# Four moves in one kernel: gate factors behind the third r tile, mixed tokens turned ahead of the S5 states, the last chunk's front half one half tile on, q tiles without the meta columns

## The chip, the cores and the metric

The kernel runs on one core of a Trainium2 chip. The metric is the device time of the whole program in microseconds (us), the median of several runs.

## What is computed

One layer of a hybrid decoder over 16 learned meta tokens, 256 prompt tokens and 8 sequences of 8 sample tokens (336 columns; 320 without the meta tokens, whose output is dropped), all in fp32:

```
xn   = rmsnorm(h) ; q, k, v, r, a, u = split(xn @ w_in)      # one input projection, width 2048 in
gk   = log_sigmoid(a @ w_gk2 + b_gk) / 16                    # GLA gates
o, S = gla_sequence(S0, q, k, v, gk)                         # chunked gated linear attention, 4 heads, dk 128, dv 256
o    = rmsnorm(o) * g_gla * silu(r)
y5   = s5_mix(u, ...)                                        # complex diagonal SSM, 64 groups
z    = gelu(y5) ; o5 = z * sigmoid(z @ w_glu + b_glu)
h    = h + concat(o, o5) @ w_out
h    = h + hier_moe(rmsnorm(h))                              # 32 experts 2048-512-2048, top 2 per token
y    = rmsnorm(h)
```

The outputs are y of prompt and sample tokens (the meta tokens' rows are dropped) and the new GLA and S5 states.

## The kernel before

Everything is laid out by hand in one SBUF array (`arena`) and one PSUM array (`ps`); each engine has its own instruction list, and semaphores order them.

**Input projection and mixers.** TensorE (PE) walks a list `TILES`: 8 u tiles, a, 4 q, 4 k, 8 v, 2 r (r0, r1), 4 gk, 6 r (r2 to r7), 8 glu. A tile is 128 output columns: `KT` = 16 weight blocks (8 for glu, 1 for gk) times all tokens, accumulated in PSUM bank p % 2. ScalarE (ACT) reads tile p out with `evacuate(p)`, and tile p + 2 waits for that. Tiles u, q, k, v have 336 columns, r and glu 320. The profile counts two PE instructions for one fp32 matmul. Weights arrive in two ring buffers of two tiles each (`load_chunk`, issued by SyncE, SP).

Between the halves of the tiles stand the steps of the S5 mixer and, from tile r5 on, those of the 11 GLA chunks (0 to 8 prompt, 9 and 10 sample; chunk 0 holds the meta tokens and gives no output). `GLA_FRONT[c]` and `GLA_BACK[c]` = front + 1 say at which half tile (2 x tile, or 2 x tile + 1) the chunk's two PE parts stand. `gla_front(c)` (L1940 to L1942) turns v and k and makes the scores; VectorE (DVE) then masks them and copies k in `front(c)` (L1452 to L1463). `gla_back(c)` (L1959, L1966, L1979) makes the output and the state updates, which DVE adds in `add_states(c)` (L1480). A sample chunk has four sequences: two updated in the back part, two in `sample_states(c, 2)` one half tile later. `gla_front(10)` waits until DVE has added all states of chunk 9. After a glu tile, DVE multiplies it into the mixed tokens with `gate_s5(i)` (L1486).

**Gates.** When gk tile 3 has been read, ACT runs `gates()`: Abs, Exp, Ln over 1408 columns; DVE takes the sums (L1411 to L1426); ACT makes `eb` and `en` (L1047, L1048); DVE takes differences (L1433 to L1437); ACT makes the last factor (L1050); DVE multiplies q and k (L1438 to L1442). All of it is one call in ACT's list, ahead of the evacuation of r2 and r3. Each change between Exp, Ln, Silu and Sigmoid costs ACT an ACT_TABLE_LOAD.

**End of the mixers.** ACT scales the ten output chunks (`scale_o`, L1066). PE turns the last S5 states `hl` (L2045, L2047), ACT copies them to `hlT` (L1107), and POOL stores them. Then PE turns the outputs chunk by chunk (L2058) and DVE multiplies them by `rT` (silu(r) times `ggla`, made at L1502) into `mixT` (L1511, 20 of them). Only then does the output projection start (L2096 and L2100, eight column blocks), with the residual rows `hrow` loaded by POOL's queue (L802 to L804) and added by DVE (L1520); PE turns h for the router between the blocks (`turn_h`, L2067, L2071).

**Experts.** The router follows. SP loads the 12 pieces of expert 0 during the output projection; each piece of a later expert is loaded when PE has used that piece of the expert before (`weights_used`, L547). All 32 experts (12 MB each) pass through the same 12 buffers (PE L2249 and L2290, DVE L1702).

Of the kernel before, what the change touches and what calls it, by code (L numbers as in the profile page):

```python
# [37 lines left out]
CL = 32  # L38
# [33 lines left out]
          + [("out", i) for i in range(8)])  # L72
CIDX = {c: i for i, c in enumerate(CHUNKS)}
COL0 = {"u": OFF_U, "q": OFF_Q, "k": OFF_K, "v": OFF_V, "r": OFF_R}
GLA_FRONT = [2 * TIDX[("r", 5)] + c for c in range(6)] + [2 * TIDX[("glu", c)] for c in range(5)]
GLA_BACK = [f + 1 for f in GLA_FRONT]


# [37 lines left out]
def bc(ap, axis, n):  # L116

    shape = list(ap.shape)
    assert shape[axis] == 1
    shape[axis] = n  # L120
    return ap.broadcast_to(shape)


def build(nc, A):
    ctx = ExitStack()
    with ctx:
# [458 lines left out]
        def _(pool):  # L585
# [90 lines left out]
            st(gp.tensor_tensor(par, p4[:, 0:2], p4[:, 2:4], ALU.add))  # L676

            for m in (qT, kT):
                st(gp.memset(m[:, 0, :, 0:PADT], 0.0))
            st(gp.memset(BP, 0.0))  # L680
            st(gp.memset(wgk, 0.0))
            st(gp.memset(wa[:, :, RANK:], 0.0))
# [204 lines left out]
        def _(act):  # L887
# [110 lines left out]
            def evacuate(p):  # L998
                kind, i = TILES[p]
                act.wait_ge(proj_done, p + 1)  # L1000
                src = ps[:, p % 2, 0:T]
                if kind == "u":
                    for q in range(4):
                        for t in range(LC):
                            u = sc.activation(U4[32 * t:32 * t + 32, i, q, :], ps[32 * q:32 * q + 32, p % 2, t:T:LC], ACT.Copy)  # L1005
                    u.then_inc(proj_read, 1)
                elif kind == "a":
                    act.wait_ge(xn_turned, 12)
                    sc.activation(aT, src, ACT.Copy).then_inc(proj_read, 1)
                elif kind in "qkv":  # L1010
                    if kind == "v" and i == 0:
                        act.wait_ge(xn_turned, 12)
                    if kind == "v":
                        h_, dst = i // 2, vT[:, i % 2].rearrange("p c (h i) -> p c h i", i=CL)
                    else:
                        h_, dst = i, qT if kind == "q" else kT
                    scale = DK ** -0.5 if kind == "q" else 1.0
                    st(sc.activation(dst[:, 0, h_, PADT:CL], src[:, 0:N_META], ACT.Copy, scale=scale))
                    sc.activation(dst[:, 1:, h_, :], src[:, N_META:].rearrange("p (c i) -> p c i", i=CL), ACT.Copy,
                                  scale=scale).then_inc(proj_read, 1)  # L1020
                elif kind == "gk":
                    act.wait_ge(scanned, 2 * NB)
                    act.wait_ge(hl_saved, 2 * NB)
                    act.wait_ge(vec_ready, 2)
                    st(sc.activation(bG[:, 0, i, PADT:CL], src[:, 0:N_META], ACT.Identity, bias=bgk[:, i:i + 1]))
                    sc.activation(bG[:, 1:, i, :], src[:, N_META:].rearrange("p (c i) -> p c i", i=CL), ACT.Identity,
                                  bias=bgk[:, i:i + 1]).then_inc(proj_read, 1)
                elif kind == "r":
                    sc.activation(rT[:, i, :], src[:, 0:TO], ACT.Silu).then_inc(proj_read, 1)  # L1029
                else:  # L1030
                    if i >= 2:
                        act.wait_ge(mix_s5, i - 1)
                    sc.activation(glu_t[i % 2], src[:, 0:TO], ACT.Sigmoid, bias=bglu[:, i:i + 1]).then_inc(proj_read, 1)

            def gates():
                act.wait_ge(rotated, 2 * NB)

                act.wait_ge(proj_read, TIDX[("gk", 3)] + 1)
                act.wait_ge(gate_b, 1)
                flat = [x.rearrange("p c h i -> p (c h i)") for x in (bG, eb, en)]  # L1040
                sc.activation(flat[2], flat[0], ACT.Abs).then_inc(gate_abs, 1)
                act.wait_ge(gate_abs, 1)
                sc.activation(flat[2], flat[2], ACT.Exp, scale=-1.0).then_inc(gate_abs, 1)
                act.wait_ge(gate_abs, 2)
                sc.activation(flat[2], flat[2], ACT.Ln, bias=1.0).then_inc(gate_abs, 1)
                act.wait_ge(gate_b, 3)
                sc.activation(flat[1], flat[0], ACT.Exp, scale=1.0 / 16).then_inc(gate_exp, 1)  # L1047
                sc.activation(flat[2], flat[2], ACT.Exp, scale=-1.0 / 16).then_inc(gate_exp, 1)  # L1048
                act.wait_ge(gate_b, 5)
                sc.activation(flat[0], flat[0], ACT.Exp, scale=1.0 / 16).then_inc(gate_exp, 1)  # L1050
# [17 lines left out]
            for p in range(len(TILES)):  # L1068
# [25 lines left out]
                    act.wait_ge(o_sqrt, 1)  # L1094
                    sc.activation(gss[:, 0:NCH - 1], gss[:, 0:NCH - 1], ACT.Sqrt).then_inc(o_sqrt, 1)
                evacuate(p)
                if TILES[p] == ("glu", 6):
                    act.wait_ge(o_rstd, 1)
                    scale_o(range(5))
                if TILES[p] == ("glu", 7):  # L1100
                    scale_o(range(5, NCH - 1))
                if TILES[p] == ("gk", 3):
                    gates()
            for i in range(2):

                act.wait_ge(hl_turned, i + 1)
                sc.activation(hlT[:, 3 * i:3 * i + 3, :], ps[:, 2 + i, 0:384].rearrange("p (a b) -> p a b", b=128),  # L1107
                              ACT.Copy).then_inc(hl_copied, 1)
# [92 lines left out]
        def _(dve):  # L1201
# [260 lines left out]
                else:  # L1462
                    ve.tensor_copy(Kexp[:, 0], ps[:, f, 256:384]).then_inc(front_ready, 1)  # L1463

            def add_states(c):
                sample = c >= NCP
                for s_ in range(SPC if sample else 1):
                    dve.wait_ge(st_done, st_count(c) + (4 * (s_ // 2) + 3 + s_ % 2 if sample else 2))
                    for h_ in range(H):
                        b_, at = state_bank(c, s_, h_)  # L1470
                        if sample:
                            dst = sstate[c - NCP][:, s_, h_]
                            dcol = eb[:, c, h_, DSEQ * s_ + DSEQ - 1:DSEQ * s_ + DSEQ]
                        else:
                            dst, dcol = S[:, h_], eb[:, c, h_, CL - 1:CL]
                        if c == 0 and h_ == 0:
                            dve.wait_ge(masks_made, 3)
                        if h_ == 0 and c >= 1:
                            dve.wait_ge(st_added, 2 * st_count(c))
                        ve.scalar_tensor_tensor(out=dst, in0=dst, scalar=dcol, in1=ps[:, b_, at:at + DV], op0=ALU.mult,  # L1480
                                                op1=ALU.add).then_inc(st_added, 1)
# [3 lines left out]
                dve.wait_ge(z_ready, 1)  # L1485
                ve.tensor_tensor(mixT[:, 8 + c, :], glu_t[c % 2], zT[:, c, :], ALU.mult).then_inc(mix_s5, 1)  # L1486

            for c in range(NCH):
                front(c)
                add_states(c)  # L1490
                kind, i = TILES[GLA_FRONT[c] // 2]
                if kind == "glu":
                    gate_s5(i)
            dve.wait_ge(o_read, NCH - 1)
            g10 = gss[:, 0:NCH - 1]
            ve.tensor_scalar(g10, g10, 1.0 / DV, EPS, ALU.mult, ALU.add).then_inc(o_sqrt, 1)
            gate_s5(5)
            dve.wait_ge(o_sqrt, 2)
            ve.reciprocal(gss[:, 16:16 + NCH - 1], g10).then_inc(o_rstd, 1)

            dve.wait_ge(proj_read, TIDX[("r", 7)] + 1)
            st(ve.tensor_tensor(rT, rT, bc(ggla.unsqueeze(2), 2, TO), ALU.mult))  # L1502
            gate_s5(6)
            gate_s5(7)
            st.sync()
            for c in range(NCH - 1):
                for hf in range(2):
# [332 lines left out]
        def _(pe):  # L1840
# [163 lines left out]
            for p, (kind, i) in enumerate(TILES):  # L2004
# [17 lines left out]
                for k in range(kt):  # L2022
# [11 lines left out]
                        mm = te.matmul(out, wgk[:, DK * i:DK * i + DK], aT, start=True, stop=True)  # L2034
                    else:
                        w = ring[n % 2][:, 0:256 * kt].rearrange("p (k n) -> p k n", n=256)[:, k, 128 * (i % 2):128 * (i % 2) + 128]
                        x = zT[:, k, :] if kind == "glu" else xnT[:, k, N_META:T] if kind == "r" else xnT[:, k, :]
                        o = out if kind not in ("r", "glu") else out[:, 0:TO]
                        mm = te.matmul(o, w, x, start=(k == 0), stop=(k == kt - 1))  # L2039
                mm.then_inc(proj_done, 1)  # L2040

            pe.wait_ge(hl_saved, 2 * NB)
            pe.wait_ge(st_added, 2 * st_count(NCH))
            for r_ in range(2):
# [3 lines left out]
                                      hl[:, r_, 1 + 4 * m:5 + 4 * m, :].rearrange("p s j -> p (s j)"), ident)  # L2048
                mm.then_inc(hl_turned, 1)

            pe.wait_ge(hl_copied, 2)
            for c in range(NCH - 1):
                pe.wait_ge(o_scaled, c + 1)
                for hf in range(2):
                    n = 2 * c + hf
                    if n >= 4:
                        pe.wait_ge(mix_gla, n - 3)
                    te.transpose(ps[:, XB[n % 4], 0:128], o_all[:, c, 128 * hf:128 * hf + 128], ident).then_inc(o_turned, 1)  # L2058

            def turn_h(i):  # L2060

                if i:
                    pe.wait_ge(hnT_ready, 2 * i)
                pe.wait_ge(h_added, 3 * i + 2)
                for k in range(2):
                    for t in range(2):
# [279 lines left out]
```

## Time and profile before

| | |
|---|---|
| median of 3 runs | 1602.82 us (1602.67 to 1604.31) |
| profiled execution | 1603.32 us, its span 1600.1 us |
| granted TensorE clock, mean | 0.882 of full speed |
| PE busy | 1263.1 us (79%) |
| DVE, ACT, POOL busy | 455.8, 255.1, 93.6 us |
| DMA | 486.60 MB, mean 304 GB/s |
| chain that ended last | PE 51%, DMA 40%, DVE 3%, issue 2%, ACT 2% |

The span runs from the first to the last instruction of the profiled execution, and its time is that of the whole program. Shares are averages over stages with different limits. The chain that ended last is followed back from the last instruction, at each step to what released it. A value in brackets behind an instruction in order of time is the idle time of its engine ahead of it and what ended that. PEld is TensorE's weight load, which overlaps its matmuls. The granted clock is a share of 2.4 GHz; its two levels are 1.2 and 2.4 GHz.

### The profile page before, as it was taken

The numbers are of one execution on the slowest core, as the hardware profiler recorded it, in microseconds if no ns is written. First come the engines' busy times: TensorE is split into PE (matmuls) and PEld (weight loads), VectorE is DVE, ScalarE is ACT, GpSimd is POOL, SyncE is SP. The second block draws the span as 40 slices with busy tenths as digits, with TensorE's granted clock in tenths as the row PEclk, the third lists the DMA queues.
The fourth block names the chain that finished last, engine by engine and source line by source line (L and its number), as shares of the span: only waits on it lengthen the run. The fifth ranks groups of instructions, "written<-read, shape, count | busy, mean of one in ns | idle before, by whom it ended". The sixth has DMA issues, their size and how long they took to land.

```text
span 1600.1 us, 17678 instructions
## 1 busy us (share of the span) xinstructions
PE 1263.1 (79%) x7026; PEld 681.2 (43%) x7026; DVE 455.8 (28%) x993; ACT 255.1 (16%) x692; POOL 93.6 (6%) x259
## 2 busy tenths in 40 slices
PE   5999999999989995866766766767766766665857
PEld 4667777765568884322222222222222222222222
DVE  4167667232430004302201201201211211201314
ACT  5452232443121112000000000000000000000012
POOL 6700000100010002000000000000000000000000
PEclk9999999999999997778878977877887887878988
DMA  9331333251379533799999999999999999999996
GB/s 214 107 106 59 100 106 102 66 156 53 106 238 368 217 106 107 315 426 429 427 428 428 428 428 428 425 428 430 418 429 428 424 430 427 422 423 426 394 426 286
DMA packets 110790, 486.60 MB, mean 304 GB/s; under 512 B 17940, under 2 KB 83288, under 8 KB 83656
## 3 DMA queue, kind: packets, MB, share of 16 engines
q1 hardware_dynamic: 107592, 473.09, 74.1%
q0 software_dynamic: 2848, 12.61, 2.4%
q8 instruction: 43, 0.70, 0.2%
q14 instruction: 19, 0.16, 0.0%
q10 hardware_dynamic: 288, 0.04, 0.0%
HBM read 478.42 MB, written 10.78 MB: 306 GB/s over the span
## 4 chain that ended last, share of the span: by engine, by line
PE 51%; DMA 40%; DVE 3%; issue 2%; ACT 2%; SPq 1%; POOL 0%; POOLq 0%; DVEq 0%; ACTq 0%
DMA arena<-in_w_up 39%; PE ps L2039 19%; PE ps L2249 11%; PE ps L2096 7%; PE ps L2195 4%; PE ps L2100 2%; PE ps L2290 1%; PE ps L1979 1%; DVE arena L1685 1%; PE ps L1914 1%; PE ps L1902 1%; SPq L547 1%; PE ps L2273 1%; DMA arena<-in_x_sample 1%; DMA hn_rows<-arena 1%
## 5 line engine op out<-in xcount | busy, mean ns | idle before, releaser
L2249 PE MATMUL ps<-arena 128*32 128x512 f32 x2048 | 321.1, 774 | 215.8 <-DMA arena<-in_w_up 214.4
L2039 PE MATMUL ps<-arena 128*128 128x336 f32 (+1 forms) x1152 | 331.1, 445 | 4.9 <-ACT arena L1029 3.6
L2249 PEld LDWEIGHTS ps<-arena 128*32 128x32 f32 x2048 | 81.2, 136 | 446.0 <-issue 445.3
L2039 PEld LDWEIGHTS ps<-arena 128*128 128x128 f32 x1152 | 216.1, 191 | 103.5 <-issue 5.8
L2290 PE MATMUL ps<-arena 128*32 128x512 f32 x1024 | 148.9, 733 | 22.7 <-DVE arena L1709 19.1
L1702 DVE COPY arena<-ps 128x512 f32<-128x512 f32 x31 | 21.3, 688 | 397.4 <-PE ps L2249 397.4
L1145 ACT ACTIVATE arena<-ps 128x128 f32<-128x128 f32 x32 | 8.9, 278 | 705.8 <-PE ps L2273 705.8
L2096 PE MATMUL ps<-arena 128*128 128x256 f32 x512 | 114.5, 382 | 0.6 <-issue 0.6
L2195 PE MATMUL ps<-arena 128*128 128x512 f32 (+3 forms) x192 | 103.0, 666 | 7.0 <-DVE arena L1685 5.1
L2096 PEld LDWEIGHTS ps<-arena 128*128 128x128 f32 x512 | 96.0, 190 | 14.9 <-issue 2.0
L1685 DVE TENSOR_TENSOR arena<-arena,ps 128x1024 f32<-128x1024 f32 (+1 forms) x48 | 58.4, 1218 | 137.1 <-PE ps L2195 137.1
L2290 PEld LDWEIGHTS ps<-arena 128*32 128x32 f32 x1024 | 39.4, 131 | 115.5 <-issue 107.7
L2273 PE MATMUL ps<-arena 128*128 128x64 f32 x256 | 66.3, 405 | 22.8 <-DVE arena L1702 22.0
L2273 PEld LDWEIGHTS ps<-arena 128*128 128x128 f32 x256 | 62.1, 327 | 41.6 <-DVE arena L1702 39.9
L1723 DVE COPY arena<-ps 32x512 f32<-32x512 f32 x62 | 42.8, 691 | 117.8 <-PE ps L2290 116.8
L1152 ACT ACTIVATE arena<-ps 32x512 f32<-32x512 f32 x62 | 36.4, 587 | 180.8 <-PE ps L2290 180.0
L2195 PEld LDWEIGHTS ps<-arena 128*128 128x128 f32 (+3 forms) x192 | 30.9, 180 | 71.7 <-issue 40.9
L872 POOL DMA_INDIRECT arena<-hn_rows,arena x7 | 7.0, 994 | 728.8 <-DVE arena L1705 728.8
L995 ACT ACTIVATE arena<-ps 32x80 f32<-32x80 f32 x128 | 39.2, 306 | 30.6 <-PE ps L1914 29.2
L1480 DVE SCALAR_TENSOR_TENSOR arena<-arena,ps 128x256 f32<-128x256 f32 x68 | 27.8, 475 | 55.4 <-PE ps L1979 55.4
L1520 DVE TENSOR_TENSOR arena<-arena,ps 128x256 f32<-128x256 f32 x16 | 6.6, 421 | 114.3 <-PE ps L2096 94.9
L1005 ACT ACTIVATE arena<-ps 32x84 f32<-32x84 f32 x128 | 29.7, 232 | 46.4 <-PE ps L2039 45.0
(387 smaller groups left out, 942.9 us busy)
## 6 DMA issues: line engine op xcount, KB each, us to landing
arena<-in_w_gate SPq DMA_DIRECT2D x62, 2048.0 KB, 18.4
arena<-in_w_up SPq DMA_DIRECT2D x62, 2048.0 KB, 22.8
arena<-in_w_down SPq DMA_DIRECT2D x62, 2048.0 KB, 22.0
arena<-in_w_in SPq DMA_DIRECT2D x16, 2048.0 KB, 9.0
arena<-in_w_out SPq DMA_DIRECT2D x8, 2048.0 KB, 8.5
arena<-in_state_gla SPq DMA_DIRECT2D x8, 512.0 KB, 9.0
arena<-in_w_glu SPq DMA_DIRECT2D x4, 1024.0 KB, 5.1
out_new_gla_sample<-arena SPq DMA_DIRECT2D x2, 2048.0 KB, 21.6
```

Of the source, the lines that this page charges most:

```text
L995: y = sc.activation(at, ps[32 * i:32 * i + 32, YB[c % 2], NCO * q:NCO * q + NCO], ACT.Copy)
L1005: u = sc.activation(U4[32 * t:32 * t + 32, i, q, :], ps[32 * q:32 * q + 32, p % 2, t:T:LC], ACT.Copy)
L1152: sc.activation(Os[CAP * i:CAP * i + CAP, 512 * x:512 * x + 512], ps[CAP * x:CAP * x + CAP, 6 + i % 2, :], ACT.Copy).then_inc(out_a, 1)
L1685: ve.tensor_tensor(d_, d_, ps[0:TR[t], b_:b_ + 2, :].rearrange("p b c -> p (b c)"), ALU.add)\
L1723: ve.tensor_copy(Os[CAP * i:CAP * i + CAP, 512 * x:512 * x + 512], ps[CAP * x:CAP * x + CAP, 6 + i % 2, :]).then_inc(out_b, 1)
L2039: mm = te.matmul(o, w, x, start=(k == 0), stop=(k == kt - 1))
L2096: mm = te.matmul(ps[:, OB[i % 2][t], 0:256], mixT[:, m, 128 * t:128 * t + 128], w[:, m, :], start=(m == 0), stop=(m == 15))
L2100: mm = te.matmul(ps[NS * x:NS * x + NS, OB[i % 2][t], 0:128], mixT[:, m, SEQ:TO], w[:, m, 128 * x:128 * x + 128], start=(m == 0), stop=(m ...
L2195: mm = te.matmul(ps[0:TR[t], b_ + x, :], Wsel[rows, 128 * t:128 * t + TR[t]], Os[rows, 1024 * j + 512 * x:1024 * j + 512 * x + 512], start ...
L2249: mm = te.matmul(ps[CAP * x:CAP * x + CAP, 0, :], xT[:, 4 * q + at, CAP * i:CAP * i + CAP], wpiece[4 * (q // 2) + 2 * up + q % 2][:, HID * ...
L2273: mm = te.matmul(ps[:, 1, at:at + 2 * CAP], GUs[:, k:HID:4], fold2.rearrange("p x t -> p (x t)"), start=True, stop=True)
L2290: mm = te.matmul(ps[CAP * x:CAP * x + CAP, 6 + i % 2, :], HT[:, k, :], wpiece[8 + k][:, 512 * x:512 * x + 512], start=(k == 0), stop=(k == 3))
```

## The change

Five edits. The gate factors (from the wait for `gate_b` on) become `gate_factors()`, called behind the evacuation of r2. Chunk 10's front part moves from the start of tile glu4 to its middle, its back part to the start of glu5, and its last states to the middle of glu5; DVE's list follows: only two sequences' states of chunk 10 ahead of the norm of the outputs, the rest behind it, and `scale_o` one tile earlier. The product of `rT` with `ggla` moves from behind the norm to behind `gate_s5(0)`. The turning of the outputs moves ahead of the turning of the S5 states, which now stands ahead of its last pair. The q tiles are computed and read for 320 columns; q of chunk 0 is set to zero.

```diff
-GLA_FRONT = [2 * TIDX[("r", 5)] + c for c in range(6)] + [2 * TIDX[("glu", c)] for c in range(5)]
+GLA_FRONT = [2 * TIDX[("r", 5)] + c for c in range(6)] + [2 * TIDX[("glu", c)] for c in range(4)] + [2 * TIDX[("glu", 4)] + 1]
...
-                st(gp.memset(m[:, 0, :, 0:PADT], 0.0))
+                st(gp.memset(m[:, 0, :, 0:CL if m is qT else PADT], 0.0))
...
+                    if kind == "q":
+                        sc.activation(qT[:, 1:, i, :], src[:, 0:TO].rearrange("p (c i) -> p c i", i=CL), ACT.Copy,
+                                      scale=DK ** -0.5).then_inc(proj_read, 1)
+                        return
...
+            def gate_factors():
+                flat = [x.rearrange("p c h i -> p (c h i)") for x in (bG, eb, en)]
                 act.wait_ge(gate_b, 3)
...
-                if TILES[p] == ("glu", 6):
+                if TILES[p] == ("glu", 5):
                     act.wait_ge(o_rstd, 1)
                     scale_o(range(5))
-                if TILES[p] == ("glu", 7):
+                if TILES[p] == ("glu", 6):
                     scale_o(range(5, NCH - 1))
                 if TILES[p] == ("gk", 3):
                     gates()
+                if TILES[p] == ("r", 2):
+                    gate_factors()
...
-            for c in range(NCH):
+            for c in range(NCH - 1):
                 front(c)
                 add_states(c)
                 kind, i = TILES[GLA_FRONT[c] // 2]
                 if kind == "glu":
                     gate_s5(i)
+                    if i == 0:
+                        st(ve.tensor_tensor(rT, rT, bc(ggla.unsqueeze(2), 2, TO), ALU.mult))
+            front(NCH - 1)
+            add_states(NCH - 1, range(2))
             dve.wait_ge(o_read, NCH - 1)
...
-            gate_s5(5)
+            gate_s5(4)
             dve.wait_ge(o_sqrt, 2)
             ve.reciprocal(gss[:, 16:16 + NCH - 1], g10).then_inc(o_rstd, 1)
-
-            dve.wait_ge(proj_read, TIDX[("r", 7)] + 1)
-            st(ve.tensor_tensor(rT, rT, bc(ggla.unsqueeze(2), 2, TO), ALU.mult))
-            gate_s5(6)
-            gate_s5(7)
+            add_states(NCH - 1, range(2, SPC))
+            for i in range(5, 8):
+                gate_s5(i)
...
-                        x = zT[:, k, :] if kind == "glu" else xnT[:, k, N_META:T] if kind == "r" else xnT[:, k, :]
+                        x = zT[:, k, :] if kind == "glu" else xnT[:, k, N_META:T] if kind in "qr" else xnT[:, k, :]
...
+            pe.wait_ge(st_added, 2 * st_count(NCH))
+            for c in range(NCH - 1):
+                pe.wait_ge(o_scaled, c + 1)
+                for hf in range(2):
+                    n = 2 * c + hf
+                    if n >= 4:
+                        pe.wait_ge(mix_gla, n - 3)
+                    te.transpose(ps[:, XB[n % 4], 0:128], o_all[:, c, 128 * hf:128 * hf + 128], ident).then_inc(o_turned, 1)
+
+            pe.wait_ge(mix_gla, 2 * (NCH - 1) - 2)
             pe.wait_ge(hl_saved, 2 * NB)
             pe.wait_ge(st_added, 2 * st_count(NCH))
...
-            pe.wait_ge(hl_copied, 2)
-            for c in range(NCH - 1):
...
                 if i:
                     pe.wait_ge(hnT_ready, 2 * i)
+                else:
+                    pe.wait_ge(hl_copied, 2)
```

## Rows read from the trace of the kernel before

**Rows 1.** Busy time per engine in three stretches; last columns clock, DMA share, GB/s.

```profile
200.00:300.00 100.00, 100.00 (x496) 72.64 (x495) 65.02 (x153) 32.12 (x111) 0.00 (x0) 1.00 0.29 89
...
500.00:550.00 50.00, 50.00 (x381) 43.35 (x378) 3.81 (x11) 5.78 (x22) 0.00 (x0) 1.00 0.87 324
...
656.00:1590.00 934.00, 655.94 (x3662) 236.52 (x3662) 185.01 (x305) 56.95 (x110) 6.96 (x7) 0.82 1.00 424
```

**Rows 2.** Chain that ended last, expert 0 and the weight stream.

```profile
650.53 3.61 PE ps L2249 x32
...
654.72 21.21 DMA arena<-in_w_up
```

**Rows 3.** Who TensorE waited for, 310 to 470 us: total, times, longest.

```profile
PE ps L2039 <- ACT arena L1029: 3.6, 1, 3.6
PE ps L1940 <- DVE arena L1480: 3.0, 1, 3.0
PE ps L2058 <- ACT arena L1107: 2.7, 1, 2.7
```

**Rows 4.** Chain that ended last, three halves of tiles of 336 columns.

```profile
119.36 13.60 PE ps L2039 x48
```

**Rows 5.** Instructions in order of time around the gates.

```profile
320.31 17.41 PE L2039 MATMUL ps<-arena 128*128 128x320 f32 x64
...
328.28 1.28 ACT L1047 ACT_TABLE_LOAD   x1
...
334.67 1.38 ACT L1047 ACTIVATE arena<-arena 128x1408 f32<-128x1408 f32 x1 [5.10 <-DVEq L1426]
...
341.20 1.62 DVE L1442 TENSOR_TENSOR arena<-arena 128x1408 f32<-128x1408 f32 x1
...
341.31 4.04 PE L2039 MATMUL ps<-arena 128*128 128x320 f32 x14 [3.60 <-ACT arena L1029]
```

**Rows 6.** Instructions in order of time, second glu tile (GLA chunk 7).

```profile
402.07 0.49 DVE L1486 TENSOR_TENSOR arena<-arena 128x320 f32<-128x320 f32 x1 [1.24 <-ACT arena L1033]
...
402.68 0.28 DVE L1463 COPY arena<-ps 128x128 f32<-128x128 f32 x1
...
404.11 0.70 PE L1979 MATMUL ps<-arena 32*128 32x256 f32 x4
```

**Rows 7.** Instructions in order of time, chunk 10 and the last glu tiles.

```profile
431.57 0.66 PE L1940 MATMUL ps<-arena 128*128 128x128 f32 x2 [2.98 <-DVE arena L1480]
...
432.66 3.47 PE L2039 MATMUL ps<-arena 128*128 128x320 f32 x8
...
443.15 1.90 PE L1979 MATMUL ps<-arena 32*128 32x256 f32 x16 [0.54 <-DVE arena L1480]
...
444.99 13.19 PE L2039 MATMUL ps<-arena 128*128 128x320 f32 x48
```

**Rows 8.** Instructions in order of time, last glu tiles to output projection.

```profile
451.03 2.76 DVE L1502 TENSOR_TENSOR arena<-arena 128x2560 f32<-128x2560 f32 x1
...
458.21 0.53 ACT L1033 ACTIVATE arena<-ps,arena 128x320 f32<-128x320 f32 x1 [1.79 <-PE ps L2039]
...
458.77 0.49 DVE L1486 TENSOR_TENSOR arena<-arena 128x320 f32<-128x320 f32 x1 [3.81 <-ACT arena L1033]
...
461.96 4.59 DVE L1511 TENSOR_TENSOR arena<-ps,arena 128x128 f32<-128x128 f32 x20 [2.70 <-PE ps L2058]
...
466.66 8.65 PE L2096 MATMUL ps<-arena 128*128 128x256 f32 x39 [0.60 <-issue]
```

**Rows 9.** Busy time per engine and granted clock in two stretches.

```profile
432.00:436.00 4.00, 4.00 (x14) 2.90 (x13) 1.79 (x6) 0.39 (x1) 0.00 (x0) 0.63 0.00 0
...
461.00:466.00 5.00, 4.25 (x20) 3.01 (x20) 4.00 (x18) 1.96 (x4) 3.28 (x6) 0.66 1.05 349
```

**Rows 10.** Instructions in order of time, first residual add and first turn of h.

```profile
485.95 0.75 DVE L1520 TENSOR_TENSOR arena<-arena,ps 128x256 f32<-128x256 f32 x2 [19.40 <-DMA arena<-in_x_sample]
...
491.29 0.60 PE L2067 MATMUL ps<-arena 128*128 128x128 f32 x4
```

More of the change, by code:

```diff
@@ L1015, in evacuate @@
                     else:
[L1016 to L1020, printed above, removed]
+                        h_, dst = i, kT
+                    st(sc.activation(dst[:, 0, h_, PADT:CL], src[:, 0:N_META], ACT.Copy))
+                    sc.activation(dst[:, 1:, h_, :], src[:, N_META:].rearrange("p (c i) -> p c i", i=CL), ACT.Copy)\
+                      .then_inc(proj_read, 1)
                 elif kind == "gk":
@@ L1463, in front, with add_states @@
                     ve.tensor_copy(Kexp[:, 0], ps[:, f, 256:384]).then_inc(front_ready, 1)
-            def add_states(c):
+            def add_states(c, which=None):
                 sample = c >= NCP
-                for s_ in range(SPC if sample else 1):
+                for s_ in which or range(SPC if sample else 1):
                     dve.wait_ge(st_done, st_count(c) + (4 * (s_ // 2) + 3 + s_ % 2 if sample else 2))
@@ L2036, in _ @@
                         w = ring[n % 2][:, 0:256 * kt].rearrange("p (k n) -> p k n", n=256)[:, k, 128 * (i % 2):128 * (i % 2) + 128]
-                        x = zT[:, k, :] if kind == "glu" else xnT[:, k, N_META:T] if kind == "r" else xnT[:, k, :]
-                        o = out if kind not in ("r", "glu") else out[:, 0:TO]
+                        x = zT[:, k, :] if kind == "glu" else xnT[:, k, N_META:T] if kind in "qr" else xnT[:, k, :]
+                        o = out if kind not in ("q", "r", "glu") else out[:, 0:TO]
                         mm = te.matmul(o, w, x, start=(k == 0), stop=(k == kt - 1))
                 mm.then_inc(proj_done, 1)
+            pe.wait_ge(st_added, 2 * st_count(NCH))
[7 more added lines that the diff above has]
+            pe.wait_ge(mix_gla, 2 * (NCH - 1) - 2)
             pe.wait_ge(hl_saved, 2 * NB)
@@ L2049, in _ @@
                 mm.then_inc(hl_turned, 1)
-            pe.wait_ge(hl_copied, 2)
-            for c in range(NCH - 1):
[L2053 to L2058, printed above, removed]
             def turn_h(i):
```

## The prediction

> **What bounds the kernel.** I began with the busy times by stretch. From 656 to 1590 us the DMA engines are full at 424 GB/s while PE is idle a third of the time; in the projections, 200 to 300 us, PE is busy throughout and the DMA engines are not, and so it is in the output projection [rows 1]. Two stages with two limits, so the next question is what ties them. The chain that ended last shows it: 32 passes of expert 0 end at 654.14, and 0.58 us later a transfer of expert 1 starts, which is on the chain for 21 us [rows 2]. The weight stream can't start before expert 0 frees its pieces, and expert 0 stands at the end of PE's list: projections, GLA, output projection, router. So a microsecond that PE gains ahead of the output projection moves the whole stream, and the end, by a microsecond; nothing gained on DVE or ACT counts unless PE waited for it. The waits of PE between 310 and 470 us are therefore the list to look at: 3.6 us for ACT's read of an r tile, 3.0 for DVE's states, 2.7 for ACT's copy of the S5 states [rows 3]. The sum below is the shift of the start of L2096, 466.66 us before [rows 8].
>
> **q tiles.** Four tiles of 16 matmuls, two passes each, go from 336 to 320 columns: 128 passes. A pass of 336 columns takes 13.60 / 48 = 0.283 us [rows 4], one of 320 columns 17.41 / 64 = 0.272 us [rows 5]; 128 x 0.0113 = 1.4 us. By columns alone it would be 0.283 x 16 / 336 x 128 = 1.7. PE is never idle in 200 to 300 us [rows 1], and the q tiles stand in the same S5 pattern, so I count it in full: 1.4, ends 0 (DVE's S5 chain sets the pace after all) and 1.7. The memset that is wider by 16 columns a head runs on POOL while PE turns x and is counted at nothing: without that cover it is a fraction of a microsecond.
>
> **Gate factors.** PE ends r3 at 320.31 + 17.41 = 337.72 and starts r4 at 341.31: 3.6 us [rows 5], the longest wait [rows 3]. r4 needs r2 read; r2 was done at 320.31 + 8.7 = 329.0, but ACT was inside the gates until the last factor at 338.1 and a table load behind it. With the new list ACT, free at 328.3, loads Silu's table (1.28, as the row at 328.28 [rows 5]), reads r2 (0.45) at 329.6 to 330.0, loads Exp's table again until 331.3, and only then waits for DVE's sums, which come at 334.67 as before. The added table load lies in that wait with 3.3 us over; without the wait it would cost 1.3. Behind it everything runs as before: last factor 338.1, r3 read at 341.3. r4 starts at 337.7, ends at 346.4; r5 needs r3 read (341.3) and the first GLA front part needs DVE's last product (341.20 + 1.6 = 342.8 [rows 5]): both are there 3.6 us or more before. Queued behind ACT's new wait is only the read of r3, which stood behind the same wait before. Gain 3.6; ends 0 and 3.6.
>
> **Product of rT.** It takes 2.76 us [rows 8]. Before, it ran from 451.03 while ACT had not yet read glu6, so taking it from there gains nothing. Behind `gate_s5(0)` it stands ahead of DVE's front part of chunk 7: gate_s5 is at 402.07, so the product runs from about 402.5 to 405.2 and the copy of k, at 402.68 before, comes 2.7 us later, ending at 405.7. PE's back part of chunk 7 started at 404.11 [rows 6] and now waits until about 405.7: a new stall of 1.6 us inside glu1, with the rest of PE's list behind it. -1.6; ends -2.8 (nothing covers it) and 0.
>
> **Chunk 10.** DVE ends chunk 9's states at about 431.4, and `gla_front(10)` starts at 431.57 [rows 7] after 3.0 us of waiting [rows 3]. Now half of glu4 (8 passes, 8 x 0.272 = 2.2 us) is put ahead of it; 0.8 us of the wait is left. So 2.2 us of work goes into the wait. The granted clock then: the front part took 432.66 - 431.57 = 1.09, and the next eight passes 3.3 us against 2.2 (0.63 granted in 432 to 436) [rows 7, 9]; in both PE came out of the 3.0 us wait at the lower level, 1.2 GHz for about 3 us. With the wait cut to 0.8 us I expect the upper level: 0.5 + 1.1 = 1.6 us back. The rest of the pattern (back part, half a tile, 0.5 us wait for DVE, four states, 443.15 to 444.99 for the last [rows 7]) keeps its length and is followed by two and a half tiles where three stood. Gain 2.2 + 1.6 = 3.8; ends 2.2 (clock still low) and 4.0. On DVE the norm's two small steps and a later `add_states` fit in front of glu5's end. ACT reads glu5 after the root and a table load, some 2 us ahead of the end of glu5, and glu7 needs it a tile later.
>
> **Turning.** glu7 ended at 444.99 + 13.19 = 458.18; L2096 started at 466.66, 8.5 us later. In between: S5 states turned (to 458.8), 2.7 us wait for ACT, which was at `scale_o` and then the copies, then 20 products on DVE in 4.6 us [rows 3, 8]. Now the outputs are scaled before glu7 ends, and the first product waits only for ACT's read of glu7 (0.56) and `gate_s5(7)` (to 459.26, 1.1 us after PE's end [rows 8]). 1.1 + 4.6 = 5.7 to the last product. The S5 states' turning (0.65 us) waits for the 18th, 0.46 us before that, so L2096 starts about 6.1 us after glu7. Gain 8.5 - 6.1 = 2.4; ends 1.0 (see the clock below) and 2.8. Its queues: SP's list here (weights of block 1, then the stores of the GLA states) hangs on glu7's end as before and passes no moved step. ACT's copy of the S5 states and POOL's six stores come 3 us later, and ahead of the residual rows in POOL's list; POOL was waiting there for the store of S anyway, and is about even with it. The first residual add was at 485.95, PE's first turn of h, which needs it, at 491.29 [rows 10]. PE comes 2.4 us earlier relative to that load: 2.9 us are left, about 2.1 after the two adds. The wait for ACT's copy of the S5 states, which stood ahead of the turning, now stands ahead of that first turn of h, some 25 us after the copy. Expert 0's pieces have the whole output projection and router to arrive.
>
> **Sum.** 1.4 + 3.6 - 1.6 + 3.8 + 2.4 = 9.6 us. The profiled execution took 1603.3 us, so one like it takes 1593.7; it lay 0.5 above the median of 1602.8, and I predict 1593.2 us for the median, 0.6% less.
>
> **The clock, row and rule.** Between 461 and 466 us the granted clock was 0.66 after PE had waited 2.7 us, and the output projection began at the upper level: 39 passes in 8.65 us, 0.22 each [rows 9, 8]. The sum takes that for after too. The Trainium skill, "TensorE: Matmul & The Clock Gate", Part 1, says that the clock is throttled by default and activity releases it; the rows at 431 and 461 us agree. By that rule the change has a weak place: ahead of L2096 PE now does nothing but turnings at DVE's pace for 6 us. By the row, 2.4 us is gained there; by the rule it may be some 1.5 less, if the low level lasts into L2096 as it lasted 3 us in [rows 7]. That is a rival.
>
> **Rivals.** *Low clock into the output projection*, or after chunk 9's states: costs 1 to 3 us, time 1594.2 to 1596.2. For it: the two low stretches [rows 9]. Against: after such a stretch L2096 started at full level. Chance 0.17. *Residual rows late*: column block 2's weights are now asked for 2.4 us earlier and share the DMA engines with the rows' last microseconds; 2 us of margin could become a stall of up to 2 us: 1593.2 to 1595.2, chance 0.06. *The r4 wait stays* (ACT enters the Exp load late or r3's read slips): 1596.8, chance 0.04. *The rT product is hidden*, because DVE reaches it earlier or PE has other work: 1591.6, chance 0.08; against it, PE's own list has nothing else at that place. *The stream gives it back*: it starts earlier but takes longer. 9.6 of 934 us is 1%, while the DMA share is already 1.00 [rows 1]; within 0.2% it would have to give back 6.4 us: 1600 to 1605, chance 0.04. *Slower*: the output projection stays at 1.2 GHz after the turnings. Each pass then costs 0.22 us more [rows 8]; 44 passes eat the 9.6 us, 58 or more give over 1606, and the projection has 512 of them and as many narrower ones. Against: the lower level lasted 3 us in both places. Chance 0.01. My forecast, all five terms within their neighbourhood (1591.7 to 1594.7), holds the remaining 0.60.
>
> The range takes in all but the last two rivals: 1590.5 to 1597. A measurement of this kernel can tell about 0.2% (3.2 us) from no change. Faster 0.94, within 0.2% 0.04, slower 0.02 (0.01 added for what I haven't seen).
>
> **What would show it.** Right: q passes of 0.272 us; r4 behind r3 without a gap, and a Silu and an Exp load between Ln and L1047; a wait of PE for DVE of about 1.6 us in glu1 and the rT product ahead of it; under 1 us ahead of `gla_front(10)`, clock 1.0 behind it; about 6 us from glu7's end to L2096; L2096 at about 457 us and expert 1's first transfers 9.6 us earlier. Wrong: a longer first wait for the residual rows, slow passes at the start of L2096, or a stream longer than 945 us from the first transfer to the end.

## The result and the profile after

The changed kernel took 1592.97 us (median of 6 runs, 1591.46 to 1595.3), the kernel before 1603.57 us in the same comparison (6 runs): ratio 0.9928, 95% interval 0.9914 to 0.9941. The profiled execution took 1591.46 us; its span is 1589.7 us, 10.4 shorter than before. Runs more than 1.5% above the fastest of their kernel count in no ratio of this document; there were two, both of rt_twice below (1688.77 and 4929.36 us, of ten).

The waits of TensorE (PE) from 305 to 465 us: total, times, longest. L2044, L2049, L2059 and L2109 are the old L2034, L2039, L2058 and L2096.

```profile
PE ps L1989 <- issue: 1.6, 1, 1.6
PE ps L1989 <- DVE arena L1488: 1.1, 2, 0.5
PE ps L2059 <- DVE arena L1521: 1.0, 1, 1.0
PE ps L2044 <- ACT arena L1032: 0.7, 1, 0.7
PE ps L1950 <- DVE arena L1488: 0.6, 1, 0.6
```

Of the three waits of [rows 3] the one of 3.6 us is gone and the one of 3.0 is 0.6. The 2.7 us for ACT's copy are gone too; in the turnings PE now waits 1.0 us for DVE's first product. The wait of 1.6 us "for issue" is new. The 0.7 us and the two of 0.5 were there before.

The q tiles, in the chain that ended last, and instructions in order of time around the gates:

```profile
119.63 12.96 PE ps L2049 x48
```

```profile
319.09 26.02 PE L2049 MATMUL ps<-arena 128*128 128x320 f32 x96
...
327.06 1.28 ACT L1032 ACT_TABLE_LOAD   x1
...
328.35 0.44 ACT L1032 ACTIVATE arena<-ps 128x320 f32<-128x320 f32 x1
328.81 1.28 ACT L1053 ACT_TABLE_LOAD   x1
...
333.41 1.38 ACT L1053 ACTIVATE arena<-arena 128x1408 f32<-128x1408 f32 x1 [3.32 <-DVEq L1434]
...
339.95 1.62 DVE L1450 TENSOR_TENSOR arena<-arena 128x1408 f32<-128x1408 f32 x1
...
344.95 0.27 PE L1950 MATMUL ps<-arena 128*128 128x128 f32 x1
```

48 passes of the q tiles take 12.96 us for 13.60 [rows 4]. From the first pass of the q tiles to the second half of the first k tile it is 48.68 us (113.26 to 161.94) where 50.38 stood (112.78 to 163.16). r2, r3 and r4 are one row of 96 passes. ACT loads Silu's table, reads r2, loads Exp's table and stands ready 3.3 us before DVE's sums let it go on, at 333.41. DVE's last product ends at 341.6, 3.4 us before the first GLA front part (344.95).

Second glu tile:

```profile
396.99 0.49 DVE L1494 TENSOR_TENSOR arena<-arena 128x320 f32<-128x320 f32 x1 [1.25 <-ACT arena L1036]
397.40 2.82 DVE L1503 TENSOR_TENSOR arena<-arena 128x2560 f32<-128x2560 f32 x1
...
400.33 0.28 DVE L1471 COPY arena<-ps 128x128 f32<-128x128 f32 x1
...
400.72 0.70 PE L1989 MATMUL ps<-arena 32*128 32x256 f32 x4 [1.62 <-issue]
```

The rT product stands between `gate_s5(0)` and chunk 7's front part, whose last copy ends at 400.6; PE had been free for 1.6 us.

Chunk 10 and the end of the glu tiles; then the way to the output projection:

```profile
425.13 2.42 PE L2049 MATMUL ps<-arena 128*128 128x320 f32 x8
...
428.18 0.41 PE L1950 MATMUL ps<-arena 128*128 128x128 f32 x2 [0.63 <-DVE arena L1488]
...
428.76 2.32 PE L2049 MATMUL ps<-arena 128*128 128x320 f32 x8
...
438.14 1.90 PE L1989 MATMUL ps<-arena 32*128 32x256 f32 x16 [0.54 <-DVE arena L1488]
...
439.97 11.03 PE L2049 MATMUL ps<-arena 128*128 128x320 f32 x40
```

```profile
451.04 0.53 ACT L1036 ACTIVATE arena<-ps,arena 128x320 f32<-128x320 f32 x1 [1.79 <-PE ps L2049]
...
451.60 0.49 DVE L1494 TENSOR_TENSOR arena<-arena 128x320 f32<-128x320 f32 x1 [3.81 <-ACT arena L1036]
452.01 4.04 DVE L1521 TENSOR_TENSOR arena<-ps,arena 128x128 f32<-128x128 f32 x20
...
452.44 3.20 PE L2059 MATMUL ps<-arena 128*128 128x128 f32 x16 [1.00 <-DVE arena L1521]
...
455.71 0.28 PE L2065 MATMUL ps<-arena 128*32 128x128 f32 x1
...
456.38 13.98 PE L2109 MATMUL ps<-arena 128*128 128x256 f32 x64
```

Eight passes of glu4 now stand ahead of chunk 10's front part, eight behind it at 0.27 us each. glu7 ends at 439.97 + 11.03 = 451.00. The first product of DVE starts 1.0 us later, 20 take 4.04 us, and the S5 states turn from 455.71 on, under the last of them.

The clock in three of these stretches (the number before the DMA share), 0.63 and 0.66 in the stretches of [rows 9]:

```profile
428.00:432.00 4.00, 3.82 (x27) 2.59 (x31) 2.22 (x8) 0.91 (x2) 0.00 (x0) 1.00 0.00 0
...
451.00:454.00 3.00, 2.00 (x13) 1.31 (x11) 2.40 (x12) 0.53 (x1) 0.00 (x0) 1.00 0.58 173
454.00:456.30 2.30, 2.23 (x15) 1.66 (x15) 2.05 (x11) 0.05 (x1) 0.00 (x0) 1.00 1.06 367
```

The first residual add and PE's first turn of h; then the weight stream:

```profile
479.37 0.75 DVE L1530 TENSOR_TENSOR arena<-arena,ps 128x256 f32<-128x256 f32 x2 [23.31 <-DMA arena<-in_x_sample]
...
480.94 0.60 PE L2080 MATMUL ps<-arena 128*128 128x128 f32 x4
```

```profile
644.19 0.39 SPq L547 DMA_DIRECT2D arena<-in_w_up  x1
...
646.00:1580.00 934.00, 649.31 (x3660) 234.10 (x3659) 185.27 (x306) 56.96 (x110) 6.96 (x7) 0.82 1.00 423
```

5.3 us stood between the two before [rows 10], 1.6 us now, 0.8 after the second add: nothing waited. The second pair of expert 1's transfers is issued at 644.19 us, before at 654.72 [rows 2]: 10.5 us earlier. The stream is as full as before [rows 1].

To compare traces I cut each profiled execution at five places that the timeline shows: the first pass of r2, PE's front part of chunk 0, the end of glu7, the start of the output projection, and expert 0's first pass. In us:

| | start to r2 | r2 to front 0 | to end of glu7 | to projection | to expert 0 | to end | span |
|---|---|---|---|---|---|---|---|
| before | 320.3 | 29.7 | 108.2 | 8.5 | 177.7 | 955.7 | 1600.1 |
| after | 319.1 | 25.9 | 106.1 | 5.4 | 177.6 | 955.8 | 1589.7 |
| gates_only | 323.2 | 25.9 | 107.9 | 8.4 | 177.6 | 955.7 | 1598.7 |
| gates_only_2 | 321.0 | 25.9 | 108.2 | 8.5 | 177.8 | 955.9 | 1597.3 |
| q_only | 318.4 | 29.8 | 108.2 | 8.5 | 177.6 | 955.9 | 1598.3 |
| chunk10_only | 321.1 | 31.4 | 104.4 | 8.0 | 177.7 | 955.2 | 1597.7 |
| turn_only | 324.2 | 32.5 | 108.8 | 5.4 | 177.6 | 956.4 | 1604.8 |
| chunk10_back | 317.8 | 25.9 | 111.5 | 5.4 | 177.6 | 956.1 | 1594.2 |
| rt_twice | 321.6 | 25.9 | 112.9 | 5.4 | 177.6 | 956.8 | 1600.1 |
| rt_hidden | 319.0 | 25.9 | 104.4 | 5.4 | 177.6 | 957.2 | 1589.4 |
| rt_hidden_hl_early | 318.9 | 25.9 | 104.4 | 5.2 | 177.7 | 960.9 | 1592.9 |
| r4_filled | 321.2 | 29.6 | 108.1 | 8.5 | 177.5 | 955.9 | 1600.8 |
| after_2 | 319.4 | 25.9 | 106.1 | 5.4 | 177.5 | 956.0 | 1590.2 |
| rt_hidden_2 | 319.9 | 25.9 | 104.4 | 5.4 | 177.6 | 956.6 | 1589.7 |

Each row is one execution, so a stage that agrees over many rows can be read to 0.1 us, and a span only to a few us. The stage from the projection to expert 0 is the same to 0.3 us in all fourteen.

### The profile page after: what moved, and what is told of

It is laid out like the page before. It is cut to its first block, busy times and chain, and to the rows that moved or that the text cites. A ratio compares the mean times of both kernels' runs of the same rounds, so it can differ in the third digit from the quotient of the medians.

```text
span 1589.7 us, 17676 instructions
## 1 busy us (share of the span) xinstructions
PE 1252.5 (79%) x7026; PEld 677.4 (43%) x7026; DVE 455.4 (29%) x993; ACT 256.4 (16%) x689; POOL 93.5 (6%) x259
## 4 chain that ended last, share of the span: by engine, by line
PE 55%; DMA 37%; DVE 3%; issue 2%; SPq 1%; ACT 1%; POOL 0%; POOLq 0%; DVEq 0%; ACTq 0%
DMA arena<-in_w_up 35%; PE ps L2049 20%; PE ps L2262 11%; PE ps L2109 7%; PE ps L2208 5%; PE ps L2303 2%; PE ps L2113 2%; DVE arena L1695 1%; PE ps L1989 1%; PE ps L2286 1%; PE ps L1924 1%; PE ps L1912 1%; DMA arena<-in_x_sample 1%; SPq L547 1%; DMA hn_rows<-arena 1%
## 5 line engine op out<-in xcount | busy, mean ns | idle before, releaser
L2049 PE MATMUL ps<-arena 128*128 128x336 f32 (+1 forms) x1152 | 328.2, 442 | 1.3 <-issue 1.3
L2049 PEld LDWEIGHTS ps<-arena 128*128 128x128 f32 x1152 | 215.3, 190 | 97.5 <-issue 3.7
L2109 PE MATMUL ps<-arena 128*128 128x256 f32 x512 | 114.4, 382 | 0.0
L2109 PEld LDWEIGHTS ps<-arena 128*128 128x128 f32 x512 | 96.0, 190 | 14.1 <-issue 1.2
L1005 ACT ACTIVATE arena<-ps 32x84 f32<-32x84 f32 x128 | 29.7, 232 | 46.4 <-PE ps L2049 45.0
```

The costliest lines, as they stand in the source:

```text
L2109: mm = te.matmul(ps[:, OB[i % 2][t], 0:256], mixT[:, m, 128 * t:128 * t + 128], w[:, m, :], start=(m == 0), stop=(m == 15))
```

## The experiments

Theory: every microsecond that PE waits or works less ahead of expert 0 comes off the end, and each part of the change is worth its own PE time. Rivals: the stream gives it back; the waits hide each other; the clock, not the wait, is what changed. The ratio behind a label is that to the kernel before on the same chip, with its 95% interval.

**Gates alone** (gates_only, gates_only_2): the kernel before with

```diff
+            def gate_factors():
+                flat = [x.rearrange("p c h i -> p (c h i)") for x in (bG, eb, en)]
                 act.wait_ge(gate_b, 3)
...
+                if TILES[p] == ("r", 2):
+                    gate_factors()
```

> The kernel before with the gate factors behind the read of r2, and nothing else of the change. My theory: r4 starts behind r3 without a gap (3.6 us before), and since nothing later in the list takes it up, the output projection, expert 1's first transfer and the end all come 3.6 to 3.9 us earlier: about 0.23% faster. Rival, the weight stream has its own start or gives the time back: the output projection starts earlier but the span stays within 1 us.

> Gate factors alone once more, beside r4_filled on one chip. My theory: the wait's 3.6 us and the clock of r4_filled together, so 4 to 6 us (0.25 to 0.37%) shorter than before, and 3.6 us shorter than r4_filled. Rival, exactly the wait: 3.6 us, and r4_filled as long as before.

0.995 (0.9933 to 0.9967), then 0.9974 (0.9961 to 0.9987). Front part 0 comes 25.9 us behind r2 in both, 3.9 us less than before, and nothing later in the table grows. The second interval, 2.1 to 6.3 us, holds the 3.9; the first (four runs), 5.3 to 10.8, lies above it, and nothing in its trace explains the excess. The second holds my 4 to 6 us and the rival's 3.6 alike, so it does not part them.

**q tiles alone** (q_only): the memset, the evacuation and the matmul lines of the change.

> The kernel before with only the q tiles cut to 320 columns. My theory: passes of 0.270 us for 0.283, 128 of them, so the gk tiles and everything behind start 1.7 us earlier and the span is 1.7 us shorter. Rival, DVE's S5 chain sets the pace between the q tiles: PE shows waits for DVE or ACT ahead of the S5 parts and the span is shorter by less than 0.5 us.

0.9992 (0.9968 to 1.0016): within noise, as 1.7 us are 0.1%. Its start to r2 is 1.9 us shorter than before's, but this stage differs by up to 3.9 us between executions with equal q tiles (table). So the size rests on the pass, (13.60 - 12.96) / 48 x 128 = 1.7 us, and on the stretch of the q tiles: 48.68 us here too (112.57 to 161.25), 1.7 less than before. The mean start to r2 is 321.8 us over the six traces with the old q tiles and 319.3 over the eight with the new: the right way, and 1.7 within that spread. The profile shows no new wait of PE between the q tiles.

**Chunk 10 alone** (chunk10_only): `GLA_FRONT`, DVE's list with `gate_s5(4)`, then the last states, then the rT product as before, then `gate_s5` 5 to 7.

> The kernel before with only chunk 10's parts half a tile on (PE's places and DVE's list; the rT product stays behind the norm, scale_o and the turnings stay). My theory: wait ahead of the front part 0.6 to 0.8 us for 3.0, granted clock 1.0 behind it, the end of glu7 3.8 us earlier. From there as before unless the rT product, now behind chunk 10's last states, delays gate_s5: span 3.5 to 3.8 us shorter. Rival, the clock does not come back: only 2.2 us, with passes of 0.53 us after the front part.

0.9977 (0.9965 to 0.9989). The interval, 1.8 to 5.6 us, holds the forecast; the rival's 2.2 is ruled out by the trace: the stage to the end of glu7 is 104.4 us, 3.8 shorter, as in the sum, with 2.2 us for the eight passes behind the front part. A by-product is in the next stage, 0.5 us shorter with the turnings unchanged: the 20 products of DVE took 4.05 us there, not 4.59 [rows 8], with PE at the upper level (granted clock 1.00, in [rows 9] 0.66).

```profile
460.71 4.05 DVE L1514 TENSOR_TENSOR arena<-ps,arena 128x128 f32<-128x128 f32 x20 [2.71 <-PE ps L2061]
...
459.70:464.70 5.00, 3.87 (x20) 2.62 (x20) 3.99 (x20) 2.01 (x4) 3.28 (x6) 1.00 1.08 352
```

**Turnings alone** (turn_only): the outputs turned ahead of the S5 states, `scale_o` a tile earlier.

> The kernel before with only the turnings exchanged and scale_o one tile earlier. My theory from the trace of after: PE stays at the upper level of the clock, the 20 products take 4.0 us for 4.6, the S5 states turn under the last of them, and the output projection starts 5.4 us after the end of glu7 for 8.5: 3.1 us shorter. Rival, the faster products in the trace of after came from something else of the change: products at 0.23 us each here too, 2.4 us shorter.

0.9972 (0.9955 to 0.9989), that is 1.8 to 7.2 us. 5.4 us from glu7 to the projection, 3.1 shorter, and 4.04 us for the 20 products: the rival with 0.23 us each falls. Together with chunk10_only this splits the term: 0.5 us from the products at the upper level, 2.6 from the order. The profiled execution was nevertheless 4.7 us longer than before's. The table says where: start to r2 (3.9) and r2 to front 0 (2.8), neither touched by this edit. Its r tiles, in order of time, and the clock behind the wait:

```profile
324.17 17.41 PE L2039 MATMUL ps<-arena 128*128 128x320 f32 x64
...
345.32 11.56 PE L2039 MATMUL ps<-arena 128*128 128x320 f32 x32 [3.74 <-ACT arena L1029]
...
345.30:350.30 5.00, 4.98 (x10) 3.18 (x11) 1.53 (x1) 0.29 (x1) 0.00 (x0) 0.50 1.09 356
```

The 32 passes of r4 behind the 3.7 us wait take 11.39 us to the front part (345.32 to 356.71), at a granted clock of 0.50 in the first 5 us, against 8.72 in [rows 5] (341.31 to 350.03), which had nearly the same wait (3.60) and a clock of 1.00. And its first u tile took 12.3 us where before's took 9.3. The same wait is followed by slow passes in one execution and not in another.

**Chunk 10 put back** (chunk10_back): the changed kernel with `GLA_FRONT` and the order of DVE's `front`, `add_states` and `gate_s5` for chunk 10 of before.

> The changed kernel with chunk 10's parts back at their places of before, all else kept. My theory: the wait of 3.0 us ahead of the front part returns, the clock falls to the lower level for about 3 us, and the span is 3.8 us longer than the changed kernel's (1593.5). Rival, clock unharmed: 2.2 us longer.

0.9937 (0.9917 to 0.9956). The stage to the end of glu7 is 111.5 us, 5.5 longer than after, more than the 3.8 I expected and far more than the rival's 2.2. The run times can't settle that size: the ratio is 0.0009 above the changed kernel's 0.9928, 1.4 us, and the two intervals together leave 3.8 us either way.

```profile
399.38 0.70 PE L1985 MATMUL ps<-arena 32*128 32x256 f32 x4 [1.62 <-issue]
...
401.90 4.01 PE L2045 MATMUL ps<-arena 128*128 128x320 f32 x8
...
428.49 0.41 PE L1946 MATMUL ps<-arena 128*128 128x128 f32 x2 [2.98 <-DVE arena L1488]
...
429.09 3.99 PE L2045 MATMUL ps<-arena 128*128 128x320 f32 x8
```

Behind the 3.0 us wait eight passes take 3.8 us where 2.2 would do (429.09 to 432.91, granted clock 0.57 from 429 to 433), so the clock falls. But eight passes behind the product's 1.6 us wait take 3.9 us as well, 1.6 more than in the changed kernel's trace. Chunk 10's own part is as expected: from the second state updates of chunk 9 to the end of glu7 it is 31.5 us, 27.7 in the changed kernel. 3.8 + 1.6 = 5.4.

**The rT product** (rt_twice, rt_hidden, rt_hidden_2): doubled in place by a product without use (first cut), and moved into a gap of DVE (second):

```diff
                     if i == 0:
                         st(ve.tensor_tensor(rT, rT, bc(ggla.unsqueeze(2), 2, TO), ALU.mult))
+                        st(ve.tensor_tensor(mixT[:, 0:8], zT, bc(ggla.unsqueeze(2), 2, TO), ALU.mult))
```

```diff
                 front(c)
+                if c == 6:
+                    dve.wait_ge(proj_read, TIDX[("r", 7)] + 1)
+                    st(ve.tensor_tensor(rT, rT, bc(ggla.unsqueeze(2), 2, TO), ALU.mult))
                 add_states(c)
...
-                    if i == 0:
-                        st(ve.tensor_tensor(rT, rT, bc(ggla.unsqueeze(2), 2, TO), ALU.mult))
```

> The changed kernel with a second product of the same size (zT by ggla, into a part of the mixed tokens that is overwritten later) right behind the rT product. The output is the reference's; the second product is work without use. My theory: PE's wait in glu1 grows by the whole 2.7 us to 4.3 and so does the span (1592.4), since PE's list ahead of expert 0 is the limit; perhaps 1 us more if the clock falls to the lower level in that wait. Rival, something behind takes it up: span within 1 us of the changed kernel.

> The changed kernel with the rT product between front(6) and add_states(6), where DVE waited 3.3 us for PE. My theory: the 1.6 us wait of PE in glu1 was all due to the product's place; it goes, and the span is 1.6 to 1.7 us shorter than that of the changed kernel (about 1588.0). Rival, the product's cost is only moved: DVE's states of chunk 6 come late and PE waits as long in the next part.

Doubled: 0.9962 (0.9948 to 0.9976). Against the changed kernel's ratio that is 5.5 us longer, 2.3 to 8.6 with both intervals: nothing behind takes it up. The stage grew by 6.9 us: the wait by 2.7, as expected, and the rest is clock. The clock behind the wait, then instructions in order of time:

```profile
405.98:414.80 8.82, 8.82 (x26) 4.47 (x27) 1.66 (x4) 0.75 (x3) 0.00 (x0) 0.50 0.01 2
```

```profile
405.98 1.22 PE L1990 MATMUL ps<-arena 32*128 32x256 f32 x4 [4.36 <-issue]
...
410.46 4.54 PE L2050 MATMUL ps<-arena 128*128 128x320 f32 x8
...
415.38 2.32 PE L2050 MATMUL ps<-arena 128*128 128x320 f32 x8
```

From 405.98 to 414.8 PE works at half speed (granted clock 0.50); the 8 passes of 2.2 us take 4.4. I had expected "perhaps 1 us" of that, and it was 4.1.

Hidden: 0.9903 (0.9882 to 0.9924).

```profile
390.48 0.28 DVE L1471 COPY arena<-ps 128x128 f32<-128x128 f32 x1
390.68 2.81 DVE L1500 TENSOR_TENSOR arena<-arena 128x2560 f32<-128x2560 f32 x1
...
394.02 1.66 DVE L1488 SCALAR_TENSOR_TENSOR arena<-arena,ps 128x256 f32<-128x256 f32 x4 [0.53 <-PE ps L1990]
```

The product fits into DVE's wait for PE's state updates, 3.3 us before; 0.5 us of it is left, the states start as before, and PE's wait in glu1 is gone: 104.4 us for 106.1 in the table, in both runs. On one chip with the changed kernel:

> The changed kernel once more, on the chip of the next. Expected: 0.6 to 0.75% shorter than before; u0, r4 and glu passes at the upper level in this profile or some 3 us more where one of them is not.

> rt_hidden once more, on the chip of the changed kernel. My theory: 1.7 us shorter than the changed kernel, and up to 1 us more in the mean, since the wait of 1.6 us in glu1 was followed by slow passes in one trace (chunk10_back). Rival: no difference that shows beyond 0.5 us.

after_2 0.9934 (0.9912 to 0.9955), median 1592.05 us; rt_hidden_2 0.9916 (0.9899 to 0.9933), median 1590.09. Both expectations of size hold in the medians: 0.66% for the changed kernel, and 2.0 us between the two, which agree with the stage's 1.7. But the intervals overlap, and the profiled spans differ by only 0.3 us (rt_hidden, after) and 0.5 us (the second pair): in both traces of rt_hidden the stretch behind expert 0's first pass is longer, 957.2 and 956.6 us for 955.8 and 956.0. It is 955.2 to 956.8 in the traces of slower kernels as well, so whether the stream gives part of these 1.7 us back, or differs by itself, is not shown.

**S5 states turned in DVE's last wait** (rt_hidden_hl_early): rt_hidden with

```diff
+                    if n == 4:
+                        pe.wait_ge(hl_saved, 2 * NB)
+                        for r_ in range(2):
+                            te.transpose(ps[0:NJ, 4 + 3 * r_, 0:128], hl[:, r_, 0, :], ident)
...
```

> The kernel rt_hidden with the S5 states turned in the 1.0 us in which PE waits for DVE's first product, into banks 4 and 7. My theory: their 0.65 us fit into that wait, the output projection starts 0.2 to 0.3 us earlier relative to glu7's end, POOL's stores and the residual rows are issued earlier; about 1.9 us shorter than the changed kernel (1587.8). Rival, the states' turning pushes the later turnings and the projection starts as late or later.

0.9903 (0.9882 to 0.9924), the same as rt_hidden beside it; a gain of 0.2 us can't be seen in a ratio. The stage is 0.2 us shorter, as expected. But the residual rows did not come earlier for PE. Instructions in order of time:

```profile
449.40 0.27 PE L2061 MATMUL ps<-arena 128*32 128x128 f32 x1
...
450.47 3.29 PE L2068 MATMUL ps<-arena 128*128 128x128 f32 x16 [0.25 <-DVE arena L1522]
...
454.27 14.05 PE L2109 MATMUL ps<-arena 128*128 128x256 f32 x64 [0.51 <-issue]
...
477.62 0.75 DVE L1531 TENSOR_TENSOR arena<-arena,ps 128x256 f32<-128x256 f32 x2 [23.45 <-DMA arena<-in_x_sample]
...
478.91 0.60 PE L2078 MATMUL ps<-arena 128*128 128x128 f32 x4
```

PE's turn of h starts 0.5 us behind the end of the first two adds, 0.8 in the changed kernel. POOL had issued its six stores by 454.4 us and then waited 5.8 us for the store of S: the rows hang on that store, which no part of this edit moves. Its profiled span is 3.5 us longer than rt_hidden's, all of it behind expert 0's first pass; one execution, and I did not find the cause.

**The wait filled** (r4_filled): six matmuls without use ahead of r4's wait, the kernel before otherwise.

```diff
+                if (kind, i) == ("r", 4):
+                    for k in range(6):
+                        te.matmul(ps[:, 2, 0:TO], xnT[:, k, 0:128], xnT[:, k, N_META:T], start=True, stop=True)
```

> The kernel before with six matmuls of 320 columns (12 passes, 3.3 us) into an unused bank ahead of r4's wait for ACT: work without use, the output is the reference's. The place of r4 is as before. My theory now: an idle wait of PE costs its length and, in part of the executions, 2 to 3 us more of passes at the lower level of the clock behind it. So with the wait filled, front part 0 is 29.7 us behind the start of r2 in every execution (29.7 to 32.5 seen before), and the mean is 0.5 to 2 us shorter than before. Rival, filling costs its own time: 1 us or more longer than before.

```profile
338.48 3.39 PE L2012 MATMUL ps<-arena 128*128 128x320 f32 x12
...
342.07 8.88 PE L2042 MATMUL ps<-arena 128*128 128x320 f32 x32 [0.20 <-ACT arena L1029]
...
350.79 0.38 PE L1940 MATMUL ps<-arena 128*128 128x128 f32 x2
```

PE waited 0.2 us in place of 3.6, and r4's passes ran at the upper level: 8.72 us to the front part. The time was 1.0008 of before (0.9992 to 1.0024). If the filling itself costs nothing (29.6 us to the front part, 29.7 before), what the clock costs behind this wait in the mean over executions is below 1.3 us: the upper part of my 0.5 to 2 is ruled out, the lower is not shown. The rival, 1 us or more longer, lies within the interval too. One profile can't show that every execution has 29.7 us. Against gates_only_2 on the same chip it is 5.5 us longer, 2.1 to 8.8 with both intervals, which holds the 3.6 expected.

## Why the prediction was right

The forecast was 1593.2 us; measured 1592.97. As a gain it was 9.6 us, against 10.6 between the medians of the one comparison, since the median of the kernel before was 1603.57 there and not 1602.82. By its own steps:

- **What bounds the kernel** holds. After the start of the projection both traces agree to 0.2 us up to the end, though everything starts 10.3 us earlier. The rival of a stream that gives it back falls for this change. So does that of waits that hide each other: each part's stretch is as long in the trace with that part alone as in the changed kernel's (48.7 us for the q tiles, 25.9 from r2 to the front part, 27.7 from chunk 9's second state updates to the end of glu7, 5.4 to the projection). The ratios say it more weakly: the parts alone, less 1.7 us for the rT product, give 0.7 to 1.0% together, the whole 0.7%.
- **q tiles**: 1.4 forecast, 1.7 measured. I took the pass of 320 columns, 0.272 us, from a row whose last end is modelled; 96 passes in 25.86 us (319.09 to 344.95) are 0.269 each. The figure by columns, which I gave as the upper end, was right.
- **Gate factors**: 3.6 forecast, 3.9 in the trace (29.72 to 25.86). The same modelled end hid 0.2 us of it: r4 started 21.0 us behind r2 [rows 5], and 64 passes of 0.269 us are 17.2. All side steps came as written: two table loads in DVE's time, r3's read and the front part on time.
- **rT product**: -1.6 forecast, -1.7 measured (from chunk 7's front part to its back part 4.5 us, 396.23 to 400.72, where 2.8 stood, 401.31 to 404.11); undone by rt_hidden. The rival that something hides it falls.
- **Chunk 10**: 3.8 forecast, 3.8 in the trace and in chunk10_only. The level of the clock came back as assumed: 0.63 became 1.00.
- **Turning**: 2.4 forecast, 3.1 measured. The main size that was off is the product: I took DVE's 0.23 us as DVE's own pace; it was PE's, whose turnings were at the lower level (0.66 in [rows 9]), and it is 0.20 with PE at the upper one, 0.55 us over 20. The S5 states turned under the last products, as forecast, but the end of the sum was rounded the wrong way: 5.7 - 0.46 + 0.65 is 5.9, not 6.1. The rival of a low clock that reaches into the output projection did not come true: 64 passes took 13.98 us (0.22 each), in all eight traces with the new order but rt_hidden_hl_early, where it was 14.05.
- **Residual rows**: not late, but I gave them 2.1 us behind the two adds and 0.8 were left: the first add came 23.0 us behind the start of the projection where 19.3 stood, 3.7 later, and I had taken off the forecast gain of 2.4.

The terms sum to 1.7 + 3.9 - 1.7 + 3.8 + 3.1 = 10.8 us at the start of the projection, of which 10.3 arrived: the stretch ahead of the q tiles was 0.5 us longer in the trace of after (the u tile that started at 84.97 starts at 85.46). The forecast said 9.6: it was 1.2 us too small in its terms, most of it in the turning. That the median of the time came out within 0.3 us of the forecast is partly luck: the stage ahead of r2 alone differs by up to 3.9 us between executions with the same q tiles.

## What to carry to other kernels

When a long weight stream hangs on the last piece of a compute-bound stage, list the waits of the engine that bounds that stage: their lengths are the gain, at the least one for one when nothing else takes their place, and each moved instruction has to be looked up in the gaps of the engine that takes it. Place a product in a gap that the trace shows (3.3 us on DVE, two steps earlier in its list) and not behind the instruction that happens to be last. Judge small edits by stages cut from the traces, since whole runs differ by more than the edit.

## What the runs showed of the hardware that was not expected

- A wait of TensorE can have a price beyond its length, and at some places not in every execution. Behind the 3.6 to 3.7 us wait ahead of r4, the stretch of 32 passes took 8.7 us (before, q_only; granted clock 1.00), 10.4 (chunk10_only; 0.67 in its first 3.9 us) or 11.4 (turn_only; 0.50 in its first 5 us). Behind the 1.6 us wait in glu1 eight passes took 2.3 us (after, after_2) or 3.9 (chunk10_back). Behind the 3.0 us wait ahead of chunk 10 they took 3.1 to 3.9 us, for 2.2 at the upper level, in all seven traces that have it. No run shows why the places differ.
- The length of the wait alone does not decide. The 2.7 us wait ahead of the turnings was followed by a granted clock of 0.66 over 5 us in five traces (before, gates_only, gates_only_2, q_only, r4_filled) and of 1.00 in chunk10_only, whose turnings are the same and where only chunk 10's place, with DVE's list around it, had changed.
- Doubling a product of 2.7 us lengthened the stage by 6.9 us, 4.1 of them slow passes behind the longer wait (granted clock 0.50).
- The first u tile took 9.3 us in eleven traces, 10.8 in gates_only and 12.3 in turn_only and rt_twice. The Trainium skill, "TensorE: Matmul & The Clock Gate", Part 1, says that the number of slow matmuls after a start differs from run to run. The durations here agree; the profile's clock column reads 1.00 over that tile in both kinds of trace and does not show it.
- VectorE's pace on products of turned blocks, 0.23 us each in the five traces with the clock at 0.66, was TensorE's clock seen through VectorE: with the clock at 1.00 it is 0.20 in the same order of turnings (chunk10_only).
